# First layer of a hybrid diffusion step on one core: sum of squares before the modulation products, table of constants in two loads

## The reference

```
m = silu(c) @ w_mod + b_mod            # 1024 x 6144, for c_ctx and for c
sh1, sc1, g1, sh2, sc2, g2 = m
h = rmsnorm(x, ln1_g) * (1 + sc1) + sh1  # x / sqrt(mean(x*x) + eps) * ln1_g ...
z = h @ w_in                             # 1024 x 3600: conv, attention, mLSTM, gates
```

## Time and profile before

| | before |
|---|---|
| median of 3 runs | 1314.57 us (1312.12 to 1317.16) |
| the profiled execution: time | 1321.63 us |
| the profiled execution: span | 1319.8 us |
| PE / DVE / ACT / POOL busy | 91% / 32% / 19% / 3% of the span |
| PE, share of the chain that ended last | 77% |
| granted PE clock, mean | 0.965 of full speed |
| DMA | 315.12 MB, mean 239 GB/s |

### The profile page before, as it was taken

How to read it: one execution, slowest core, us unless ns; L and a number is a source line. 1 busy time by engine, 2 the same in 40 slices (tenths; PEclk the granted TensorE clock), 3 DMA queues, 4 the chain that set the end, 5 groups by cost and what they waited for, 6 DMA issues and landing times.

```text
span 1319.8 us, 15381 instructions
## 1 busy us (share of the span) xinstructions
PE 1203.8 (91%) x6254; PEld 632.7 (48%) x6254; DVE 427.1 (32%) x1185; ACT 249.7 (19%) x511; POOL 41.0 (3%) x64
## 2 busy tenths in 40 slices
PE   4799999899989989999889999989998998999994
PEld 3346555586453434343344555557645353434332
DVE  1602032336441242323261203135544125232226
ACT  1210121232231101111041012124222110111102
POOL 1500000000020000000000000000000000000000
PEclk8899999999989899999989999999998989999997
DMA  9936433393319979999771553233520998999971
GB/s 352 314 116 242 148 128 128 142 338 112 127 43 373 410 297 367 402 390 400 312 255 64 190 201 128 102 113 138 136 104 1 389 374 318 362 412 374 413 287 48
DMA packets 95366, 315.12 MB, mean 239 GB/s; under 512 B 5964, under 2 KB 6208, under 8 KB 86464
## 3 DMA queue, kind: packets, MB, share of 16 engines
q1 hardware_dynamic: 91712, 306.43, 61.0%
q0 software_dynamic: 3584, 7.71, 2.2%
HBM read 310.92 MB, written 4.99 MB: 239 GB/s over the span
## 4 chain that ended last, share of the span: by engine, by line
PE 77%; DVE 9%; DMA 9%; ACT 2%; issue 2%; SPq 0%; DVEq 0%; ACTq 0%
PE ps L872 15%; PE ps L1205 14%; PE ps L882 8%; PE ps L1247 7%; DMA ring<-in_w_up 6%; PE ps L1040 5%; PE ps L1107 5%; PE ps L831 3%; PE ps L1133 3%; PE ps L1157 1%; PE ps L821 1%; DMA ring<-in_w_mod 1%; PE ps L1134 1%; PE ps L992 1%; DVE xT L1785 1%
## 5 line engine op out<-in xcount | busy, mean ns | idle before, releaser
L1205 PE MATMUL ps<-ring,arena 128*64 128x512 f32 x816 | 242.8, 603 | 9.3 <-DMA ring<-in_w_up 9.2
L872 PE MATMUL ps<-ring,hT 128*128 128x512 f32 (+1 forms) x480 | 194.9, 565 | 0.0
L1785 DVE SCALAR_TENSOR_TENSOR xT<-ps,modT,xT 128x128 f32<-128x128 f32 x320 | 115.4, 412 | 233.7 <-PE ps L1134 172.8
L872 PEld LDWEIGHTS ps<-ring,hT 128*128 128x128 f32 x480 | 90.5, 190 | 98.0 <-issue 94.7
L1247 PE MATMUL ps<-ring,arena 128*64 128x512 f32 x384 | 115.0, 605 | 8.1 <-ACT arena L1486 8.1
L1205 PEld LDWEIGHTS ps<-ring,arena 128*64 128x64 f32 x816 | 66.3, 136 | 105.4 <-issue 105.4
L1205 PE MATMUL ps<-slot,arena 128*64 128x512 f32 x208 | 103.2, 610 | 9.8 <-DVE xT L1785 4.5
L882 PE MATMUL ps<-hT,ring 128*128 128x384 f32 x320 | 106.2, 489 | 0.0
L1040 PE MATMUL ps<-mixT,ring 128*128 128x384 f32 x256 | 83.4, 487 | 1.5 <-ACT mixT L1437 1.5
L882 PEld LDWEIGHTS ps<-hT,ring 128*128 128x128 f32 x320 | 59.8, 190 | 40.7 <-issue 0.8
L1980 DVE SCALAR_TENSOR_TENSOR y_low<-ps,route,y_high 128x512 fp32r<-128x512 f32 x32 | 24.0, 751 | 138.1 <-ACT y_high L1490 137.3
(11 more groups left out here) (307 smaller groups left out, 1287.6 us busy)
## 6 DMA issues: line engine op xcount, KB each, us to landing
ring<-in_w_up SPq DMA_DIRECT2D x56, 1024.0 KB, 10.5
ring<-in_w_gate SPq DMA_DIRECT2D x54, 1024.0 KB, 13.3
ring<-in_w_down SPq DMA_DIRECT2D x52, 1024.0 KB, 10.2
ring<-in_w_mod SPq DMA_DIRECT2D x24, 2048.0 KB, 12.5
ring<-in_w_in SPq DMA_DIRECT2D x14, 2048.0 KB, 9.1
slot<-in_w_down SPq DMA_DIRECT2D x16, 1024.0 KB, 8.7
slot<-in_w_gate SPq DMA_DIRECT2D x14, 1024.0 KB, 13.0
slot<-in_w_up SPq DMA_DIRECT2D x12, 1024.0 KB, 9.9
```

The lines of the kernel that those rows point to most:

```text
L872: mm = pe.matmul(p[:, 0:n], hT[:, k, t * P:(t + 1) * P], w[:, k, c0:c0 + n], start=(k == 0), stop=(k == KT - 1))
L1205: mm = pe.matmul(out[which][64 * s:64 * s + 64, :], xg[:, k, cols[s]], w[i][:, k % 4, :], start=(k == 0), stop=(k == KT - 1))
L1785: ins = dve.scalar_tensor_tensor(xT[:, m, cols], p[:, cols], modT[:, L, gate0 + m, j:j + 1], xT[:, m, cols], ALU.mult, ALU.add)
```

## The change

In the table of constants, the identity, the matrix of 1/1024, and the columns `eps` and `one` come first (258 columns, `C_FIRST`), the masks, selectors, rotary tables and all else behind them. SP loads the first 258 columns where it loaded the whole table, and issues the other 2053 columns behind the fourth weight of the first layer; both count on `const_loaded`, and PE waits for the second one after the modulation products, ahead of `gates`.

In the first layer PE runs `sum_squares(0)` ahead of `mod(0, 0)` to `mod(0, 3)`. DVE copies the gate weights, adds up the squares, takes the reciprocal and scales all 8 tiles (`scale`) before it takes up `mod(0, 3)`; then it waits for `mod_ready` and shifts the latent parts (`shift_latent`). ACT waits for `mod_ready` after the root, ahead of its gains and shifts. In all other norms the order of instructions is as it was, except that DVE now takes the reciprocal before it waits for `mod_ready`, and not after.

```diff
+C_IDENT, C_MEAN = 0, P
+C_EPS = 2 * P
+C_ONE = C_EPS + 1
+C_FIRST = C_ONE + 1
...
-            sp.dma_start(cst[:], a["constants"]).then_inc(const_loaded, 16)
+            sp.dma_start(cst[:, 0:C_FIRST], a["constants"][:, 0:C_FIRST]).then_inc(const_loaded, 16)
...
+                    if ly.first and i == RING - 1:
+                        sp.dma_start(cst[:, C_FIRST:], a["constants"][:, C_FIRST:]).then_inc(const_loaded, 16)
...
+                sum_squares(0)
+                if ly.first:
                     pe.wait_ge(csil_ready, 1)
                     for c in range(4):
                         mod(0, c)
-                sum_squares(0)
+                    pe.wait_ge(const_loaded, 32)
...
                     drain(("ss", n), act.activation(std[:], p[:, 0:NT], ACT.Sqrt, bias=eps))
+                    act.wait_ge(mod_ready, 2 * L + n + 1)
...
+                def scale(n, k):
+                    dve.tensor_tensor(hT[:, k, :], xT[:, k, :], std[:], ALU.mult).then_inc(ly.scaled_ready, 1)
+
+                def shift_latent(n, k):
+                    cols = STREAMS[1][1]
+                    if k not in LATENT_ON_ACT:
+                        dve.wait_ge(ly.scaled_ready, n * KT + k + 1)
+                        dve.tensor_scalar(hT[:, k, cols], hT[:, k, cols], gains[:, L, n, k, 1:2],
+                                          modT[:, L, 24 * n + k, 1:2], ALU.mult, ALU.add).then_inc(ly.h_dve, 1)
...
                     bk.wait_drained(dve, ("ss", n))
+                    link(dve.reciprocal(std[:], std[:]))
+                    if n == 0 and ly.first:
+                        for k in range(KT):
+                            scale(n, k)
+                        for c in range(4):
+                            mod(0, c)
                     dve.wait_ge(mod_ready, 2 * L + n + 1)
-                    link(dve.reciprocal(std[:], std[:]))
...
                     dve.sem_inc(vT_ready, 1)
-                    for c in range(4):
-                        mod(0, c)
```

More of the change, by code:

```diff
@@ L48 @@
 RELBIAS_DIFFS = 7
-C_IDENT, C_MASKF, C_MASKB, C_TRI, C_IOTA, C_ONES, C_MEAN = (P * i for i in range(7))
-C_SEL = 7 * P
+C_IDENT, C_MEAN = 0, P
+C_EPS = 2 * P
+C_ONE = C_EPS + 1
+C_FIRST = C_ONE + 1
+C_MASKF, C_MASKB, C_TRI, C_IOTA, C_ONES = (C_FIRST + P * i for i in range(5))
+C_SEL = C_FIRST + 5 * P
 C_ROPE = C_SEL + 8 * P
@@ L60 @@
 C_JOB = C_THRESH + 5
-C_EPS = C_JOB + OVERFLOW
-C_ONE = C_EPS + 1
-C_WIDTH = C_ONE + 1
+C_WIDTH = C_JOB + OVERFLOW
 V_LN1, V_LN2, V_BMOD, V_CONV, V_N0, V_C, V_FINAL, V_ROWS = 0, 8, 16, 64, 70, 78, 94, 102
@@ L203, in place_products @@
         spread(("vec", 0), ("vec", 1))
+    spread(("ss", 0))
+    if layer == 0:
         for c in range(4):
             mod(0, c)
-    spread(("ss", 0))
     before_heads = (0, 1, 2, 3, 4)
@@ L1559, in sum_square @@
                                       ).then_inc(ly.summed_ready, 1)
+                def scale(n, k):
[6 more added lines that the diff above has]
+                                          modT[:, L, 24 * n + k, 1:2], ALU.mult, ALU.add).then_inc(ly.h_dve, 1)
                 def norm(n):
                     bk.wait_drained(dve, ("ss", n))
+                    link(dve.reciprocal(std[:], std[:]))
[4 more added lines that the diff above has]
+                            mod(0, c)
                     dve.wait_ge(mod_ready, 2 * L + n + 1)
-                    link(dve.reciprocal(std[:], std[:]))
-                    cols = STREAMS[1][1]
                     for k in range(KT + 1):
[L1568 to L1574, removed]
+                        if k < KT and (n == 1 or not ly.first):
+                            scale(n, k)
+                        if k > 0:
+                            shift_latent(n, k - 1)
                 def gates():
```

## The result

Timed in turns, the changed kernel took 1311.54 us (median of 19 runs, 1304.19 to 1318.67), the kernel before 1319.07 (median of 19, 1312.12 to 1325.09): ratio 0.9943, 95% interval 0.9924 to 0.9963. Two things are apart in this: the level, which the first three runs of the kernel before had shown 4.5 us too low, and the gain, which is 2.7 us smaller.

What follows compares the result with a forecast made beforehand. PE has 77% of the chain; up to 56.59 us the start is a relay. Earlier data 1.1, work off the path 6.9 and padding's clock 2.1 sum to 10.2 us off 1314.57: 1304.4 us, range 1300 to 1310.

Steps and rivals of the forecast that it cites:

- the one from the profiled execution to the absolute number: Whole kernel: profiled 1321.63 us would become 1311.4; being 7.1 above the median 1314.57, the same difference gives 1304.4.
- some 2 us for the scatter of a median of three: Whole kernel's time: allowance added to gains of 6 to 12 us, giving the range 1300 to 1310.
- Earlier data: Start: with most of the table behind, x lands at 10.7, and it and the weights come 1.1 us earlier.
- the floor by SP's issue: Load of x: issued at about 4.5 behind small vectors, it can land at about 10.3 at best.
- bound by its weights alone: Fourth modulation product: waits only for its weights, runs 33.3 to 35.3, so moving the squares first costs nothing.
- the forecast's own signs of being wrong: Fourth product starting behind the third, first w_in product waiting for a load, or 56.59 becoming 46 without the span following.
- Work taken off the path: Ahead of the gates: padding starts right behind the transposes, no longer behind the sum product, 6.9 us less.
- The padding's clock: Ten padding passes before the gates: at full clock they take 4.4 us where they took 6.56, 2.1 us more gain.
- Load five: Weights mq for the first w_in product: landed at 43.1, wanted by PE at 46.4, margin 3.3 us.
- rival 1: Shared DMA after the gates: mq or the table's second half 1.2 us late; both, median 1306.8; 24% with another rival.
- rival 2: Start: PE's clock stays at half through products, padding and gates, 2.6 us later than 56.59, 1317.2, slower; 4%.
- Rival 4: Later stretches: gain given back, being bound by DMA or POOL's loads; median 1314.6; 6%.

Runs made afterwards that it cites:

- the split alone: The kernel before with only the constants table loaded in two parts, order of work as before: ratio 0.9991 to the kernel before.
- the order alone: The changed kernel with the table in one load, so only the new order of work: ratio 0.9928 to the kernel before.
- scalings late: The changed kernel, but DVE scales the 8 tiles after the gains, in one loop with the shifts: 1308.43 us, ratio 0.9934 to the kernel before.
- one matmul of padding: The changed kernel with x issued first, POOL's gate loads after x, and two padding passes in the first layer: 1304.29 us, ratio 0.9922 to the kernel before.
- the gate loads behind x: The changed kernel with x issued ahead of the nine vectors and POOL's small gate loads held until x landed: 1308.64 us, ratio 0.993 to the kernel before.
- gates without padding: The changed kernel without the ten padding passes ahead of the first layer's gates: 1305.86 us, ratio 0.9917 to the kernel before.
- the kernel with x first: The changed kernel with x's two loads issued right behind the table's first part, ahead of nine vectors: 1308.27 us, ratio 0.9914 to the kernel before.
- all three: The changed kernel with x issued first, POOL's gate loads after x, no first-layer padding: 1303.82 us, ratio 0.9901 to the kernel before; again 1306.52, 0.9932.

## Why the prediction was wrong

**Level and scatter.** Of the 7.1 us by which the forecast missed, 4.5 are the level and 2.7 the gain; the gain alone would have stayed within its bounds of 6 to 12. The step that put the time outside its range is the one from the profiled execution to the absolute number: the kernel before was set at 1314.57 and "some 2 us for the scatter of a median of three" were allowed. Nineteen runs of it have a median of 1319.07, with a standard deviation of 4.0 us; three of them can be 4.5 off, and were. The scatter is not made in the start (it varies by 1.5 us) but in the rest, by up to 10 us from profile to profile. It goes with the clock: over the 37 timed runs of the changed kernel time and mean granted clock have a correlation of -0.83 (the higher the clock, the shorter), and the profile with the shortest span (1302.3) has 0.977, that with the longest (1313.0) 0.969. As a ratio the forecast was 1304.4/1314.57 = 0.9923, just outside the first interval (0.9924 to 0.9963).

**Earlier data, forecast 1.1 us.** This term of the gain failed, in two steps. The first is x: it landed at 11.50 on the mean and not 10.7, 0.5 before the kernel before (12.04). The forecast had put the floor by SP's issue at 10.3, from an issue-to-bytes delay; the 1.2 us from there to 11.50 are as long as the stretch from 5.1 to 6.3 in which POOL's queue took 99.6% of the DMA engines with its gate load, just when x was due. The forecast had no such load in its sum. That it is the cause is read from its place; no run moved it alone. The hole from 2.8 to 5.1 is the very time that was to be gained; moving the issue filled it (x at 8.79).

The second is the sentence that the fourth product is bound by its weights alone, "33.3 to 35.3". The weights did come 0.8 earlier (33.39 on the mean for 34.19; three of four at 33.1, where 33.3 was forecast), though no run shows by which half of the change: they came at 34.02 with the split alone and at 34.17 with the order alone. The product did not follow. In three of four profiles it began right behind the third (33.2, 33.3 and, 0.9 us after its weights, 34.0), stopped after two matmuls for 0.8 to 1.2 us and went on only at 34.6 to 35.2; with all four it went on 0.5 later than before (34.70 for 34.23), not 1.1 earlier. That the product would start behind the third and not behind its weights was the first of the forecast's own signs of being wrong.

**Work taken off the path, 6.9 us.** Right: in the changed kernel padding starts at the transposes' end (38.24, and 37.61 + 0.63), where in the earlier trace rows 6.95 lay between. The parts were right too: sum product done at 26.7 (forecast 25.7 plus the x that did not come), DVE free ahead of the fourth product, tiles shifted under the padding. Scalings moved or not, the sum is the same within 0.4 us (scalings late).

**The padding's clock, 2.1 us.** Right in kind: 4.29 in all four profiles of the changed kernel, forecast 4.4, against 6.05 on the mean before: 1.8 us.

**A term that was missing.** I took the fourth product at 2.0 us on both sides, from the earlier trace rows. In the kernel before it was 3.68, at half clock, in three profiles of four. There PE stands still for 1.6 to 3.4 us ahead of the third product and for 1.8 to 3.5 ahead of the fourth. In the first profile the clock rose at 32.2, near the end of the third product, and stayed up over 1.9 us of idle; in the second and the fourth it was at half when the third product ended and stayed there; in the third it fell in the 3.5 us of idle. In the changed kernel the first three products run together, the clock is up when they end, and PE then stands still for 1.3 us at most: 1.98 to 2.10 each time. Running together is not enough: with one matmul of padding and with the gate loads behind x the three ran together too, the fourth weights came 3.0 and 2.0 us after their end, and the fourth product took 3.29 and 3.56. The difference of the two kernels is 1.3 us on the mean, and 0.2 more in the transposes behind it (1.10 for 0.64 in two profiles of the kernel before). On this the trace of the profile I had was the rare case. The Trainium skill, "TensorE: Matmul & The Clock Gate", section "Why this matters for your kernels", advises against long idle gaps between bursts of matmuls because the clock falls in them. The third profile of the kernel before agrees (half clock behind 3.5 us of idle). The gates without padding do not: there the clock fell in a gap of 1.2 us, shorter than those the page warns of.

Together: -0.5 + 6.9 + 1.8 + 1.3 + 0.2 = 9.7 us, all of the start's gain, where 10.2 was forecast. That the two are so near is luck: two errors (1.6 too much for the data, 1.5 missing for the clock) nearly cancel.

**Start against times.** The means of all times of the three sets of turns with both kernels lie 7.4 us apart (1317.9 over 59 runs, 1310.5 over 37), with an uncertainty (95%) of about 1.5 by their standard deviations of 3 to 4. The start says 9.7. Some 2 us are not accounted for: either something small is given back in the expert stages, or the few profiles differ from the timed runs. This stays open.

**The rivals.** Load five was never late: no wait for w_in in any run, even where PE wanted it at 41.9 (rival 1). The clock did not stay low (rival 2): in the changed kernel's first profile it rose after some 4 us of unbroken work. POOL and the second part of the table (landing at 18.3 + 18.1 = 36.4, PE there at 38.2) held nothing. (In the kernel before POOL's first bytes flowed at 40.7, 4.0 us after its first issue and not 3.3 as I had read; that only adds to the margin.) Rival 4 (the gain is given back later) is not seen in the rests of the spans, but for up to the 2 us that stay open.

## What to carry to other kernels

Taking bytes out ahead of a load helps only as far as the load is already issued and nothing else takes its engines; look at the DMA share in the stretch and at whose queue has it: if a hole opens there, move the issue. When independent work is moved into a stretch of waiting, read what it does to the gaps of the matrix engine, since part of what it brings may be clock (here 3.3 of 9.7 us). A gap of an engine that the profile labels "issue" is not a wait for data; look for when the data landed before you call it one. And a start, or any stretch, should be read from several profiles of both kernels before a term is sized by it: here the one profile at hand held a product at full clock that ran at half in three others.

## What the runs showed of the hardware that was not expected

- The DMA engines were busy (share 1.09) while moving 79 GB/s from 5.1 to 6.3 us, nearly all of it for the gate load of POOL (1024 pieces of 64 bytes). Its 16 packets took 1.19 us each on the mean there, and 0.18 us each in the kernel with x first, where they came at 7 us.
- PE stopped for 0.4 to 1.2 us after two matmuls of the fourth product in five profiles, its weights landed, each time shortly after a 16 KB packet of instructions had been moved.
- x, issued first (at 1.64), landed at 8.79, 9.22, 7.84, 7.99 and 8.25 in kernels that differ little: a scatter of 1.4 us that no edit here explains.
- The clock fell in a gap of 1.2 us ahead of the gates in one kernel (0.94, then 0.53) and stayed at 1.00 across a gap as long in another (all three, gates in 5.46).
